# A paced table copy, and one block's expert work split over two stages, in a streaming encoder layer on one Trainium2 core

## The reference

```python
h = rmsnorm(x, norm_mix)
qa, ka, va, qb, kb, vb, rg, ga, gb = project(h, w_in, b_gate)     # (tokens, 1024) @ (1024, 5888)
oa = sliding_window_attention(qa, ka, va, sinks)                  # 8 heads, chunks of 64, window 128
ob = retention(qb, kb, vb)                                        # 4 heads, carries a state along the stream
mix = sigmoid(ga) * (oa @ w_branch_a) + sigmoid(gb) * (retention_output(ob, rg) @ w_branch_b)
x1 = x + mix @ w_out
h2 = rmsnorm(x1, norm_ffn)

# PEER: 8 heads pick 16 of 16384 experts each, so 128 experts for each token
s1, s2 = scores(h2 @ w_q, sub_k1, sub_k2)                         # 128 keys each
best, idx = top16 of (top16(s1) + top16(s2)); gate = softmax(best)
act = gelu(h2 . expert_u[idx])                                    # one dot of 1024 elements per expert
y = rmsnorm(x1 + sum_k gate_k * act_k * expert_v[idx_k], norm_final)
```

## Time and profile before

| | |
|---|---|
| median of 3 runs | 4420.11 us (4410.85 to 4426.94) |
| the profiled execution | 4409.17 us |
| its span, first to last instruction | 4407.6 us |
| mean granted TensorE clock | 0.907 |
| PE, DVE, ACT, POOL busy | 75%, 56%, 24%, 42% |
| moved by the DMA engines | 1552.96 MB, mean 352 GB/s |

### The profile page before, as it was taken

The page is one execution under the profiler, slowest core; times in us unless marked ns, Lnnn a source line. Parts: engine busy times, 40 slices in busy tenths (PEclk is TensorE's granted clock), DMA queues, the critical chain, the costliest instruction groups (busy, mean ns, idle before and its releaser), DMA issues.

```text
span 4407.6 us, 32479 instructions
## 1 busy us (share of the span) xinstructions
PE 3313.6 (75%) x8957; PEld 1651.8 (37%) x8957; DVE 2481.5 (56%) x4999; ACT 1047.2 (24%) x2847; POOL 1860.9 (42%) x1668
## 2 busy tenths in 40 slices
PE   8666289899926767634987887887887887777776
PEld 5443156556624434312433332333332332222222
DVE  0122055987338777744575675675675675675544
ACT  2101011011112211110333333333333332332322
POOL 0032025776125455510445445445445445445554
PEclk9876599999957877767999999999999999999999
DMA  5698987999388888851999999999999999999998
GB/s 217 218 334 315 320 270 303 395 386 369 140 345 329 298 314 336 295 195 73 370 414 421 420 418 421 404 417 421 407 418 422 404 419 422 418 411 421 422 419 356
DMA packets 301854, 1552.96 MB, mean 352 GB/s; under 512 B 31217, under 2 KB 58865, under 8 KB 179185
## 3 DMA queue, kind: packets, MB, share of 16 engines
q0 software_dynamic: 239616, 1342.28, 77.0%
q1 hardware_dynamic: 47488, 187.83, 11.0%
q10 hardware_dynamic: 14592, 21.10, 1.3%
HBM read 1507.98 MB, written 178.52 MB: 383 GB/s over the span
## 4 chain that ended last, share of the span: by engine, by line
DMA 25%; PE 16%; issue 6%; DVE 3%; ACT 1%; POOL 1%; ACTq 0%; POOLq 0%; DVEq 0%
DMA ring<-uv_d,IXD_p 25%; PE ps L1460 14%; PE ps L1430 3%; DVE ring L1661 2%; POOL ring L1778 1%; ACT dg L1510 1%; ACT GE_p L1504 0%; DVE BV_p L926 0%; DVE ACC L1642 0%; DVE DOT_p L1661 0%; DVE BP_p L931 0%; ACTq L1509 0%; PE ps L1445 0%; PE ps L1423 0%; POOLq L1774 0%
## 5 line engine op out<-in xcount | busy, mean ns | idle before, releaser
L1460 PE MATMUL ps<-ring,dg 128*128 128x512 f32 x3584 | 1699.7, 611 | 455.2 <-ACT dg L1510 432.7
L1778 POOL DMA_INDIRECT ring<-uv_d,IXD_p x896 | 1120.2, 1250 | 1308.3 <-PE ps L1460 1011.4
L1661 DVE CUSTOM_DVE_ANT_0 ring<-ring,H 128x1024 f32<-128x1024 f32 x896 | 1094.6, 1224 | 878.2 <-DMA ring<-uv_d,IXD_p 862.8
L1460 PEld LDWEIGHTS ps<-ring,dg 128*128 128x128 f32 x3584 | 651.5, 192 | 1381.7 <-ACT dg L1510 711.0
L1137 PE MATMUL ps<-w,xg 128*128 128x368 f32 x1792 | 563.6, 476 | 22.4 <-issue 20.2
L1504 ACT ACTIVATE GE_p<-DOT_p 128x2 f32<-128x2 f32 x448 | 91.1, 203 | 1473.3 <-DVE DOT_p L1661 1473.3
L1137 PEld LDWEIGHTS ps<-w,xg 128*128 128x128 f32 x1792 | 342.7, 191 | 242.9 <-issue 30.8
L1510 ACT ACTIVATE dg<-gdi,GE_p 128x128 f32<-128x128 f32 x896 | 310.7, 394 | 55.0 <-PE ps L1460 7.2
L1498 ACT ACTIVATE gdi<-ident,GD_p 128x128 f32<-128x128 f32 x896 | 303.3, 386 | 14.8 <-issue 14.6
L225 POOL DMA_DIRECT2D uv_d<-in_peer_u x128 | 69.4, 543 | 495.1 <-issue 253.9
L1260 POOL DMA_INDIRECT rv<-in_peer_v,IXD x128 | 156.9, 1226 | 260.2 <-DVE AC L1242 229.9
(11 more groups left out here) (364 smaller groups left out, 2718.0 us busy)
## 6 DMA issues: line engine op xcount, KB each, us to landing
uv_d<-in_peer_u POOLq DMA_DIRECT2D x128, 512.0 KB
uv_d<-in_peer_v POOLq DMA_DIRECT2D x128, 512.0 KB
w<-in_w_in SPq DMA_DIRECT2D x8, 2944.0 KB
w<-in_w_in SPq DMA_DIRECT2D x16, 1472.0 KB
z_d<-zo ACTq DMA_DIRECT2D x16, 1288.0 KB
ring<-uv_d,IXD_p POOLq DMA_INDIRECT x896
gates_p<-z_d SPq DMA_DIRECT2D x7, 1536.0 KB
wq_s<-in_peer_w_q SPq DMA_DIRECT2D x8, 1024.0 KB, 13.2
```

The costliest lines, as they stand in the source:

```text
L1460: mm = T.matmul(bank(6 + n), dg[:, k % DR, :], ring[:, k % RS, D + n * 512:D + (n + 1) * 512], start=(k == 0), stop=(k == NK - 1))
L1661: V.tensor_tensor_reduce(out=row, in0=row, in1=H2[:], scale=1.0, scalar=0.0, op0=ALU.mult, op1=ALU.add, accum_out=DOT[:, k:k + 1]).then_in ...
L1778: g.indirect_dma_start(ring[:, n % RS, :], None, uv_d, bass.IndirectOffsetOnAxis(ap=IXD[:, n:n + 1], axis=0)).then_inc(s_ring[n % RS], 16)
```

## The change

- `pool_table` is written out instead of looping, and before piece p POOL waits until piece p - 2 has landed (one semaphore for even and one for odd pieces). So at most two pieces are under way.
- The pieces are dealt anew: 22 in stage 2 (was 32), 18 in stage 3 (was 30), 20 at the begin of stage 4 (was 24) and 12 at its end, behind all gathers of the stage, 56 in stage 5 (was 42), two behind each group.
- Of the 128 places of block 1, the first 48 run at the end of stage 4 (`dve_experts_ahead`), through the same ring of 16 rows. Their sum is stored to DRAM and loaded again in stage 5, which has the other 80 places. It has four points in a block instead of six; point 0 stands behind the softmax instead of ahead of the scores.
- In stage 4 the gates of block 0 are computed before eviction 4 (was 12), those of block 1 before 56 (was 70), gelu g of block 0 before eviction 9 + 10 g (was 16 + 12 g). The three gelus of block 1 stand before evictions 92 and 100 and behind the last.

```diff
-TABLE_BS, TABLE_E, TABLE_CS = 32, 62, 86
+TABLE_BS, TABLE_E, TABLE_S, TABLE_CS = 22, 40, 60, 72
+AHEAD = 48
...
-            with g.Fori(lo, hi) as part:
-                g.dma_start(uv_d[bass.ds(part * P, P), 0:D], rows(t["peer_u"], part)).then_inc(s_uv, 16)
-                g.dma_start(uv_d[bass.ds(part * P, P), D:], rows(t["peer_v"], part)).then_inc(s_uv, 16)
+            for part in range(lo, hi):
+                if part >= 2:
+                    g.wait_ge(s_uv[part % 2], 32 * (part // 2))
+                    g.sem_inc(s_pool, 1)
+                g.dma_start(uv_d[part * P:(part + 1) * P, 0:D], rows(t["peer_u"], part)).then_inc(s_uv[part % 2], 16)
+                g.dma_start(uv_d[part * P:(part + 1) * P, D:], rows(t["peer_v"], part)).then_inc(s_uv[part % 2], 16)
...
-            dve_point(v, blk, 0)
             v.wait_ge(s["scores"], blk + 1)
...
             dve_probs(v, blk, 2 * P)
+            dve_point(v, blk, 0)
             dve_point(v, blk, 1)
-            dve_point(v, blk, 2)
...
-            dve_point(v, blk, 3)
+            dve_point(v, blk, 2)
...
-            dve_point(v, blk, 4)
-            dve_point(v, blk, 5)
-            if blk == NB - 1:
-                dve_point(v, blk, 6)
+            dve_point(v, blk, 3)
...
+        ORDER1 = [("u", 0), ("u", 1), ("v", 0), ("u", 2), ("v", 1), ("v", 2)]
...
+        def dve_experts_ahead(v):
+            v.wait_ge(s_h2, 32)
+            v.wait_ge(d["gtc"], 3)
+            base = 2 * NK + RING
+            for n in range(2 * AHEAD):
+                kind, grp = ORDER1[n // UG]
...
+                row = ring[:, n % RING, :]
+                v.wait_ge(s_ring[n % RING], USES * 16 + 16 * (n // RING + 1))
...
-            GATES_AT, GATES1_AT = 12, 70
+            GATES_AT, GATES1_AT = 4, 56
             def gelu_at(n):
-                return (n - 16) // 12 if 16 <= n < 16 + 12 * PH and (n - 16) % 12 == 0 else None
+                return (n - 9) // 10 if 9 <= n < 9 + 10 * PH and (n - 9) % 10 == 0 else None
...
+                        if tile == WT - 2:
+                            sp.wait_ge(c["scc"], 3)
+                            sp.dma_start(H2A, rows(h2_d, 1)).then_inc(s_h2, 16)
...
+                    sp.wait_ge(d["freed"], RING + 2 * NK + 2 * AHEAD)
+                    sp.dma_start(ac_d, ACCA).then_inc(s_ac, 16)
+                    sp.wait_ge(s_ac, 16)
                     sp.wait_ge(d["yo"], 1)
...
+                        if n in (92, 100):
+                            act_gelu(act, 1, (n - 92) // 8)
...
+                    act_gelu(act, 1, 2)
                     act_norm(act, 0)
...
                     dve_experts(v, 0, True)
+                    dve_experts_ahead(v)
+                    dve_norm(v, 0)
...
-                    pool_table(g, TABLE_E, TABLE_CS)
+                    pool_table(g, TABLE_E, TABLE_S)
                     g.wait_ge(c["v1"], 3)
                     g.sem_inc(d["pool"], 1)
-                    pool_gathers(g, 0)
+                    pool_gathers(g, 0, ORDER, IXD)
+                    pool_gathers(g, 1, ORDER1, IXD1)
+                    pool_table(g, TABLE_S, TABLE_CS)
-        PG = 3
-        SET = 6 * PG
-        SETS = NK // SET
+        PG, PTS = 3, 4
+        SET = PTS * PG
+        SETS = (NK - AHEAD) // SET + 1
+        REST = NK - AHEAD
...
+                    sp.dma_start(AC1[:], ac_d).then_inc(s_ac, 16)
...
-                        for j in range(7 if blk == NB - 1 else 6):
-                            grp = 6 * (blk - 2) + j
-                            if blk > 2 and j < 6:
-                                pool_values(g, grp - 6)
+                        for j in range(PTS):
+                            grp = PTS * (blk - 2) + j
+                            if blk > 2:
+                                pool_values(g, grp - PTS)
                             pool_dots(g, grp)
-                            if TABLE_CS + grp < NEXP // P:
-                                pool_table(g, TABLE_CS + grp, TABLE_CS + grp + 1)
-                    for grp in range(LAST - 6, LAST + 1):
+                            pool_table(g, TABLE_CS + 2 * grp, TABLE_CS + 2 * grp + 2)
+                    for grp in range(LAST, TAIL):
                         pool_values(g, grp)
```

More of the change, by code:

```diff
@@ L900, in act_norm, with pool_gathers @@
             S.activation(m4[:, 2:3], m4[:, 1:2], ACT.Sqrt).then_inc(d["sq"], 1)
-        def pool_gathers(g, blk):
+        def pool_gathers(g, blk, order, index):
             g.wait_ge(d["ixd"], blk + 1)
             g.sem_inc(d["pool"], 1)
-            for n in range(2 * NK):
-                kind, grp = ORDER[n // UG]
+            for n in range(len(order) * UG):
+                kind, grp = order[n // UG]
                 if n % 4 == 0:
@@ L1071, in dve_experts @@
             V.scalar_tensor_tensor(X1[:], ACC[:, 0], m4[:, 3:4], nf[:], ALU.mult, ALU.mult).then_inc(d["yo"], 1)
+        def dve_experts_ahead(v):
[4 more added lines that the diff above has]
+                kind, grp = ORDER1[n // UG]
+                k = grp * UG + n % UG
+                if kind == "v" and n % UG == 0:
+                    cols = slice(grp * UG, (grp + 1) * UG)
+                    v.wait_ge(d["gelu"], PH + grp + 1)
+                    V.tensor_tensor(WG[:, cols], GE[:, cols], GD1[:, cols], ALU.mult).then_inc(d["wgt"], 1)
+                    v.wait_ge(d["wgt"], PH + grp + 1)
+                row = ring[:, n % RING, :]
+                v.wait_ge(s_ring[n % RING], USES * 16 + 16 * (n // RING + 1))
+                if kind == "u":
+                    V.tensor_tensor_reduce(out=row, in0=row, in1=H2A, scale=1.0, scalar=0.0, op0=ALU.mult,
+                                           op1=ALU.add, accum_out=DOT[:, k:k + 1]).then_inc(d["freed"], 1)
+                    if n % UG == UG - 1:
+                        v.wait_ge(d["freed"], base + n + 1)
+                        v.sem_inc(d["act"], 1)
+                elif k == 0:
+                    V.tensor_scalar(ACCA, row, WG[:, k:k + 1], None, ALU.mult).then_inc(d["freed"], 1)
+                else:
+                    v.wait_ge(d["freed"], base + n)
+                    V.scalar_tensor_tensor(ACCA, row, WG[:, k:k + 1], ACCA, ALU.mult, ALU.add).then_inc(d["freed"], 1)
         with ExitStack() as m:
@@ L1085, in trunk_kernel @@
             SC1 = sb(m, "SC1_s", [P, 16, NKEY])
+            H2A, ACCA = [SC1[:, 8 * i:8 * i + 8, :].rearrange("p k n -> p (k n)") for i in range(2)]
             PB = NB - 2
@@ L1764, in _ @@
                 def _(g):
-                    g.wait_ge(s_uv, 32 * (NEXP // P))
-                    g.sem_inc(d["pool"], 1)
+                    for i in range(2):
+                        g.wait_ge(s_uv[i], 32 * (NEXP // P // 2))
+                        g.sem_inc(d["pool"], 1)
                     with g.Fori(FB, NB) as blk:
```

64 lines of the change are left out of this document (33 added, 31 removed).

## The result

The changed kernel takes 4347.4 us (median of 4 runs, 4341.2 to 4351.0), the kernel before beside it 4420.1 (4410.9 to 4426.9): a ratio of 0.983, with a 95% interval of 0.981 to 0.985. In the profiled executions the spans are 4339.4 and 4407.6 us, 68 us apart; the forecast had 106.

What follows compares the result with a forecast made beforehand. No engine bounded the whole: outstanding copies held stage 3's end, PE's projection stage 4, DVE's order and gather waits stage 5. -14 - 40 + 36 - 88 = -106 from 4409.2 gave 4303; median forecast 4310, range 4255 to 4375.

Steps and rivals of the forecast that it cites:

- Stage 2, -14: Stage 2: 22 pieces end at 299 to 310 us, so wo loads alone and PE starts earlier; -14 us (8 to 18).
- Stage 3, -40: Stage 3: 18 pieces end 110 to 119 us into it, so the wait at its end goes; -40 us (36 to 43).
- A paced piece, 3.5 to 4 us: Copy of the table: with two pieces under way, a reissue barely fits into the other piece's 3.5 us; 3.5 to 4 us each.
- rival 3: Copy in stages 2 to 4: the pace costs its overlap, a piece takes 5.5 us; kernel 4394 us, chance 0.05.
- Stage 4, +36: Stage 4: block 1's rows and 12 uncovered pieces lengthen its end to 1257 against 1221.4; +36 us (+20 to +55).
- some 30 us of stall lie in them; I keep those: Stage 4's evictions: 5.2 us each against PE's own pace of 4.9; some 30 us of stall taken as unchanged.
- Stage 5, -88: Stage 5: six places fewer and fewer waits for rows, a block 84 us against 93.8; -88 us (-40 to -125).
- rival 1's lock: Stage 5: POOL stands in the copy's wait while a freed buffer could be filled; at 6 us a group 4478 us, chance 0.07.
- rival 2: Stage 5: mixers stay bound by transfers, a block near 91 us, gain 38 instead of 88; kernel 4360 us, chance 0.13.
- its own sign of being wrong: Stage 4: a length of over 770 us would show the prediction wrong; 725 to 760 us was expected.
- Rivals: Four alternatives for the whole kernel: 4478, 4360, 4394 and 4253 us, with chances 0.07, 0.13, 0.05 and 0.12.

Runs made afterwards that it cites:

- no pace: Changed kernel without the waits that hold the copy to two pieces under way, numbers and places of pieces kept: 4306.6 us, ratio 0.978.
- the changed kernel's second profile: The changed kernel run once more, unaltered, as yardstick: 4335.9 us, ratio 0.982 to the kernel before.
- with and without the copy: Changed kernel with stage 5's 56 pieces issued behind its last gathers: 4491.8 us in all, 79.3 us a block instead of 82.8.
- half rows: Changed kernel with each gather of stage 4 fetching half a row, the ring's other half zeroed by DVE beforehand: 4324.9 us, ratio 0.980.

## Why the prediction was right, and where it wasn't

- **Stage 2, -14: right,** -13, by the mechanism named: wo has the transfers to itself. The 22 pieces ended at 309 us (forecast 299 to 310). It comes without the pace too (no pace: 169.0 us, as long as the changed kernel's second profile).
- **Stage 3, -40: right,** -41. The last store lands and the stage ends at 463.7; POOL's last piece landed at 463.3. The 35.5 us at the meeting are gone because 18 pieces are fewer than 30; without the pace the stage is as short (116.6).
- **A paced piece, 3.5 to 4 us: right.** From the first issue to the last landing, 22 pieces took 3.9 us each in stage 2 and 18 took 3.9 in stage 3; the 20 at stage 4's start were issued every 3.7. The rule of the Trainium skill (DMA: Bandwidth & Descriptors, Anatomy of one DMA) that a GpSimd transfer has a fixed cost beside its bytes came into no sum. Two pieces under way covered it but for 0.3 us: a piece took 3.9 us with the pace and 3.6 in stage 2 without it, and rival 3 with its 5.5 us didn't come.
- **Stage 4, +36: the mis-sized term,** +87. The chain was the right one (gelu 7, row 80 of block 1, the last gather, the copy) and its last part too (60 us from the last gather to the end, forecast 62). Two of its terms were off, and the first is the step that failed: "some 30 us of stall lie in them; I keep those". They became 61.9, because a stall wasn't a fixed property of the projection but a price of the gathers beside it, and the change let these run earlier, without the pauses that late gates and gelus had forced on them. Work on block 0 ended at 1051.7 instead of 1021 (1075 less 54), behind gelu 7 at 1029.0, which was forecast for 997 to 1001. And h2 of block 1 was taken as there when wanted; it cost 15.2 us in SP's line. 31 + 15 of the 51 missing us, and 5 us weren't traced further. The kernel before with early gates shows the first term by itself: +38 us to the last eviction, and +30 in the median. The size of the term is that of one profile; the same program had 80.9 in another.
- **Stage 5, -88: right in mechanism, -103.** A block takes 82.8 us (forecast 84), DVE waits 5.7 us for the scores as forecast and 12 for rows (forecast 9; (41.3 + 30.5) / 6). Of the 15 us more, some 5 each came from block 2 (block 3 begins its scores 95.2 us into the stage and not 105.6, a gain of 10.4 instead of 5), from the steps between the blocks 3 to 8 (54 instead of 49), and from block 8 with the tail (39 instead of 34). POOL waited only 8 us for the copy in blocks 3 to 8, so rival 1's lock didn't come; rival 2 is refuted by the block time with and without the copy.
- **The total.** Its sum gives 4303 + 11 = 4314 for the median, and not the 4310 that it states. The kernel takes 4347.4, inside the forecast's own bounds of 4270 to 4350 by 3 us. That is in part luck: stage 4 lost 51 us more than forecast and stage 5 won 15 more. And a stage 4 of over 770 us was its own sign of being wrong, which came.
- **Rivals.** None came.

## What to carry to other kernels

A queue of transfers that another engine had been pausing by accident has a price when it is let run: before moving a wait away, ask who was undisturbed because of it, and try the early start alone. Check in whose line a moved transfer stands, not only what it moves. And a stall that is found in a profile may be kept in a sum as a constant only if what makes it is known.

## What the runs showed of the hardware

Beside POOL's runs of gathers issued back to back, one every 1.25 us, ACT waited 10 to 30 us for signals of matmuls. It was so in all twelve profiles without the pauses that have runs of 13 or more, at full rows (390 to 400 GB/s in the stretches above) and, four times, at half rows (164 GB/s of gathers). A break of 0.7 us in each four gathers took it away at 381 to 396 GB/s, and holding the gathers to 8 took it away at 332 to 353. What holds the signals up in the chip, no run here shows; nor why 30 of the 86 such runs had no wait of over 10 us beside them, nor what made the 24% of these waits that lie outside them. A stage didn't end before POOL's outstanding copies: in the changed kernel POOL was through 9 to 11 us behind its last issue in each stage, and a tail of 12 pieces cost 58 us from its first issue.
